# The running sum of the value rows in PSUM in the second pass, with 58 rows of the first kind ahead

## What is computed

```python
def peer(h, w_pq, sub_keys, u_tab, v_tab):
    ...
        expert = i0 * PEER_NKEYS + i1
        g = jax.nn.softmax(c_top, axis=-1)
        u = u_tab[expert]
        a = jax.nn.gelu(jnp.einsum('bthkd,btd->bthk', u, hb, preferred_element_type=jnp.float32),
                        approximate=False)
        return jnp.einsum('bthk,bthkd->btd', (g * a).astype(v_tab.dtype), v_tab[expert])
```

## Time and profile before

| | |
|---|---|
| median of 3 runs | 1715.59 us (1715.45 to 1722.47) |
| the profiled execution | 1718.16 us, its span from first to last instruction 1716.3 us |
| PE / DVE / POOL / ACT busy over the span | 88% / 68% / 41% / 28% |
| TensorE clock granted, mean | 0.966 |
| first pass | about 503 to 999 us |
| second pass | about 999 us to the end; gathered units from 1018 us |
| HBM read | 628.91 MB over the span |

### The profile page before, as it was taken

The page is one execution under the profiler, slowest core; times in us unless marked ns, Lnnn a source line. Parts: engine busy times, 40 slices in busy tenths (PEclk is TensorE's granted clock), DMA queues, the critical chain, the costliest instruction groups (busy, mean ns, idle before and its releaser), DMA issues.

```text
span 1716.3 us, 28250 instructions
## 1 busy us (share of the span) xinstructions
PE 1513.2 (88%) x11065; PEld 1412.6 (82%) x11065; DVE 1159.2 (68%) x1798; ACT 486.8 (28%) x1402; POOL 698.2 (41%) x420
## 2 busy tenths in 40 slices
PE   9999999999999999999999998777777776766766
PEld 7768888889999999999999998766777766766766
DVE  5335695767789999148676737666666666676766
ACT  6557567656540000034445481000000000000000
POOL 2020000000013222111001018888888888888885
PEclk9999999999999999999999999999888989999998
DMA  9664446476669999989999989998999999997887
GB/s 347 229 137 144 136 136 198 138 240 198 241 203 422 421 421 422 418 340 402 384 352 385 339 282 338 360 341 306 340 346 326 332 339 331 324 326 255 287 302 264
DMA packets 115092, 517.21 MB, mean 301 GB/s; under 512 B 25937, under 2 KB 28113, under 8 KB 62625
## 3 DMA queue, kind: packets, MB, share of 16 engines
q0 software_dynamic: 57488, 293.87, 47.0%
q1 hardware_dynamic: 48176, 156.19, 26.2%
q10 hardware_dynamic: 9360, 66.35, 9.7%
HBM read 628.91 MB, written 3.41 MB: 368 GB/s over the span
## 4 chain that ended last, share of the span: by engine, by line
PE 51%; POOL 17%; DMA 16%; issue 10%; DVE 4%; ACT 1%; POOLq 0%; DVEq 0%; SPq 0%; ACTq 0%
PE ps L1551 19%; DMA late<-in_u_tab 5%; PE ps L1335 5%; PE ps L1340 5%; PE ps L1337 5%; POOL late L498 5%; PE ps L1606 4%; POOL raw L516 3%; DMA late<-in_v_tab,acts 3%; POOL late L516 3%; POOL late L496 3%; DMA raw<-in_u_tab 3%; PE ps L1357 2%; POOL acts L498 2%; PE ps L1499 2%
## 5 line engine op out<-in xcount | busy, mean ns | idle before, releaser
L1606 PE MATMUL ps<-acts,raw 128*128 (+1 forms) x2048 | 266.7, 295 | 89.8 <-DMA raw<-in_v_tab,acts 89.5
L1606 PE MATMUL ps<-acts,late 128*128 (+1 forms) x2048 | 262.8, 291 | 90.4 <-DMA late<-in_v_tab,acts 90.4
L1606 PEld LDWEIGHTS ps<-acts,raw 128*128 128x128 f32 x2048 | 257.9, 209 | 98.1 <-issue 94.0
L1606 PEld LDWEIGHTS ps<-acts,late 128*128 128x128 f32 x2048 | 253.4, 205 | 98.4 <-issue 97.0
L846 DVE TENSOR_TENSOR w_lo<-raw,w_hi 128x512 fp32r<-128x512 f32 (+1 forms) x288 | 188.8, 682 | 131.3 <-ACT w_hi L540 129.7
L1161 DVE SCALAR_TENSOR_TENSOR late<-late,acts 128x2048 f32<-128x2048 f32 x85 | 194.2, 2293 | 96.6 <-DMA late<-in_u_rows,sel 95.8
L1165 DVE SCALAR_TENSOR_TENSOR acts<-late,sel,acts 128x2048 f32<-128x2048 f32 x85 | 200.2, 2355 | 65.4 <-DMA late<-in_v_tab,acts 61.8
L1551 PE MATMUL ps<-acts,late 128*128 128x128 f32 x2048 | 239.1, 276 | 5.6 <-DMA late<-in_u_tab 5.5
L1551 PEld LDWEIGHTS ps<-acts,late 128*128 128x128 f32 x2048 | 233.0, 192 | 8.4 <-DMA late<-in_u_tab 5.2
L1551 PE MATMUL ps<-acts,raw 128*128 128x128 f32 x1984 | 231.2, 276 | 3.1 <-DMA raw<-in_u_tab 2.8
L1551 PEld LDWEIGHTS ps<-acts,raw 128*128 128x128 f32 x1984 | 225.6, 192 | 5.8 <-DMA raw<-in_u_tab 4.7
(11 more groups left out here) (218 smaller groups left out, 1825.5 us busy)
## 6 DMA issues: line engine op xcount, KB each, us to landing
raw<-in_w_in SPq DMA_DIRECT2D x72, 512.0 KB, 3.7
late<-in_u_tab SPq DMA_DIRECT2D x33, 1024.0 KB, 10.8
raw<-in_u_tab SPq DMA_DIRECT2D x32, 1024.0 KB, 10.7
late<-in_u_tab ACTq DMA_DIRECT2D x31, 1024.0 KB, 10.8
raw<-in_u_tab ACTq DMA_DIRECT2D x30, 1024.0 KB, 10.5
raw<-in_w_o SPq DMA_DIRECT2D x32, 512.0 KB, 4.2
raw<-in_w_pq SPq DMA_DIRECT2D x32, 512.0 KB, 3.5
raw<-in_w_in SPq DMA_DIRECT2D x8, 400.0 KB, 3.4
```

Of the source, the lines that this page charges most:

```text
L1606: ins = mm(ps[:, pair_bank(k // 2), at:at + N_DN], ring[q][:, k * P:k * P + P], acts[:, ds(i * (4 * N_DN) + q * N_DN, N_DN)], start=first ...
```

## The change

The running sum moves from `acc` in SBUF to `held`, banks 0 to 3 of PSUM (2048 float32 per partition). The first value row reads `acc` and writes `held`; the last reads `held` and writes `acc`; the 126 between read and write `held`. The products of the rows of the first kind are written to SBUF as before. `U_FIRST` is 58 for 48, so that all rows ahead of the second pass are of the first kind; then 70 and 70 alternate, and 58 value rows stand at the end. PE's results of the second pass lie in banks 4 to 7 alone, 512 columns in each (`out_bank`), so that the first unit no longer waits in its middle; the copies, transposes and last sums go by banks, 4 for 8.

```diff
-        U_FIRST = 48
+        U_FIRST = 58
         ROWS = [("u", n) for n in range(U_FIRST)]
         for n in range(U_FIRST, N_PICK):
             ROWS += [("u", n), ("v", n - U_FIRST)]
         ROWS += [("v", n) for n in range(N_PICK - U_FIRST, N_PICK)]
         U_LAST = [ROWS.index(("u", TOPK * h + TOPK - 1)) for h in range(NH)]
         ROWS_U = 58
+        V_ROW = [ROWS.index(("v", n)) for n in (0, N_PICK - 1)]
...
-        def pair_bank(p):
-            return (p + 4) % 8
+        def out_bank(b):
+            return ps[:, 4 + b, :]
+
+        held = ps[:, 0:4, :].rearrange("p b n -> p (b n)")
...
             for n in range(4):
-                sp.wait_ge(out_ready, 2 * n + 2)
+                sp.wait_ge(out_ready, n + 1)
...
-            for p in range(KD // 2):
-                act.wait_ge(pair_mm, p + 1)
-                nc.scalar.activation(outT[:, 2 * p:2 * p + 2, :], ps[:, pair_bank(p), 0:2 * N_DN].rearrange("p (k t) -> p k t", k=2),
-                                     ACT.Copy).then_inc(outT_done, 1)
+            for b in range(KD // 4):
+                act.wait_ge(bank_mm, b + 1)
+                nc.scalar.activation(outT[:, 4 * b:4 * b + 4, :], out_bank(b).rearrange("p (k t) -> p k t", k=4), ACT.Copy).then_inc(outT_done, 1)
...
                         dve.wait_ge(row_used, r)
-                        V.scalar_tensor_tensor(acc, row[r % NROW], w_sp[:, n:n + 1], acc, ALU.mult, ALU.add).then_inc(row_used, 1)
+                        V.scalar_tensor_tensor(acc if r == V_ROW[1] else held, row[r % NROW], w_sp[:, n:n + 1], acc if r == V_ROW[0] else held, ALU.mult, ALU.add).then_inc(row_used, 1)
...
             apply(NKEY - 1)
 
+            dve.wait_ge(gelu_done, NKEY)
             next_row(3)
...
-            for p in range(KD // 2):
-                dve.wait_ge(outT_mm, p + 1)
-                cols = slice(256 * p, 256 * p + 256)
-                V.tensor_tensor(o_rest[:, cols], ps[:, pair_bank(p), 0:256], x_rest[:, cols], ALU.add).then_inc(out_ready, 1)
+            for b in range(KD // 4):
+                dve.wait_ge(outT_mm, b + 1)
+                cols = slice(512 * b, 512 * b + 512)
+                V.tensor_tensor(o_rest[:, cols], out_bank(b), x_rest[:, cols], ALU.add).then_inc(out_ready, 1)
...
                 for k in range(KD):
-                    if first and k == 8:
-                        pe.wait_ge(gelu_done, NKEY)
-                    at = N_DN * (k % 2)
-                    ins = mm(ps[:, pair_bank(k // 2), at:at + N_DN], ring[q][:, k * P:k * P + P], acts[:, ds(i * (4 * N_DN) + q * N_DN, N_DN)],
-                             start=first and k % 2 == 0, stop=last and k % 2 == 1)
+                    at = N_DN * (k % 4)
+                    ins = mm(out_bank(k // 4)[:, at:at + N_DN], ring[q][:, k * P:k * P + P], acts[:, ds(i * (4 * N_DN) + q * N_DN, N_DN)],
+                             start=first and k % 4 == 0, stop=last and k % 4 == 3)
```

More of the change, by code:

```diff
@@ L252, in build_block @@
         expert_in, used_done, unit_ready = sem("expert_in"), sem("used_done"), sem("unit_ready")
-        pair_mm, outT_done, outT_mm = sem("pair_mm"), sem("outT_done"), sem("outT_mm")
+        bank_mm, outT_done, outT_mm = sem("bank_mm"), sem("outT_done"), sem("outT_mm")
         out_ready, out_sent = sem("out_ready"), sem("out_sent")
@@ L1588, in _, with out_transposes @@
             pe.wait_ge(gated, N_GRP)
[L1589 to L1593, removed]
+            def out_transposes(b):
+                pe.wait_ge(outT_done, b + 1)
+                for k in range(4):
+                    ins = nc.tensor.transpose(out_bank(b)[:, P * k:P * k + P], outT[:, 4 * b + k, :], ident[:, :])
                 ins.then_inc(outT_mm, 1)
@@ L1602, in v_chunk @@
                 for k in range(KD):
-                    if first and k == 8:
-                        pe.wait_ge(gelu_done, NKEY)
-                    at = N_DN * (k % 2)
-                    ins = mm(ps[:, pair_bank(k // 2), at:at + N_DN], ring[q][:, k * P:k * P + P], acts[:, ds(i * (4 * N_DN) + q * N_DN, N_DN)],
-                             start=first and k % 2 == 0, stop=last and k % 2 == 1)
-                    if last and k % 2:
-                        ins.then_inc(pair_mm, 1)
-                        if k >= 5:
-                            out_transposes(k // 2 - 2)
+                    at = N_DN * (k % 4)
+                    ins = mm(out_bank(k // 4)[:, at:at + N_DN], ring[q][:, k * P:k * P + P], acts[:, ds(i * (4 * N_DN) + q * N_DN, N_DN)],
+                             start=first and k % 4 == 0, stop=last and k % 4 == 3)
+                    if last and k % 4 == 3:
+                        ins.then_inc(bank_mm, 1)
+                    if last and k in (9, 13):
+                        out_transposes(k // 4 - 2)
                 if not last:
@@ L1626, in _ @@
                 v_chunk(NKEY // 4 - 1, q, last=q == 3)
-            for p in range(KD // 2 - 2, KD // 2):
-                out_transposes(p)
+            for b in range(KD // 4 - 2, KD // 4):
+                out_transposes(b)
     return nc
```

## The result

The changed kernel takes 1592.5 us in the median (1588.1 to 1594.0), the kernel before beside it 1719.0. The ratio is 0.926, 95% interval 0.922 to 0.929: **7.4% faster**. Forecast were 1626 us and a range of 1590 to 1690, so the time lies in it, 2.5 us above its lower edge; the gain is 127 us where 93 were forecast.

What follows compares the result with a forecast made beforehand. POOL's issue rate was taken to bound the second pass; freed, DMA's 388 and DVE's 142 us make 530, with 12% loss 594. 1018 + 594 + 15 = 1627, forecast as a 1626 us median, range 1590 to 1690.

Steps and rivals of the forecast that it cites:

- The bound of before: Second pass, from 1018 us: POOL's issue rate bounds it, 320 instructions at one per 2.15 us.
- What holds POOL: Gathers issued inside DVE row instructions: a second SBUF input holds them; the changed sum has none, freeing 168 us of POOL.
- 1.40 us a row instruction: Second pass: each DVE product or sum with two SBUF inputs costs POOL 1.40 us over undisturbed gathers.
- The sum in PSUM for nothing: Value rows' sums on DVE: PSUM in place costs nothing, 2.44 us each; bounds 2.44 and 4.5 us.
- The rival with half of the rate: Sums in place in PSUM run at half rate, 4.5 us each, making DVE the bound: 1777 us, chance 0.06.
- The 65 ns more: Skill's higher fixed cost for PSUM on DVE: 65 ns x 128 = 8 us, doubted from the trace's 687 against 686 ns.
- What is late next: Second pass with POOL freed: DMA bounds the alternating part, 388 us, DVE the end, 142; 530 us together.
- the 12% for four servers that stall one another: Second pass: loss added to 530 us because POOL, DMA, DVE and PE stall each other, giving 594; bounds 5 to 20%.
- better than summed: Rival: losses under 5% and a full PE clock; at 4% 551 us for the second pass, 1583 in all; chance 0.06.
- The tail: End of the kernel, behind the second pass: 15 us, taken from 1701 to 1716 us of the kernel before.
- DMA early at 364 GB/s: Rival: DMA takes POOL's place in the second pass at a 364 GB/s ceiling, 1675 us, chance 0.16.
- Order, `gelu_done`, four banks: 58 rows ahead move nothing in the first pass; the gelu_done wait costs nothing; four output banks 0 to +1 us, taken as 0.

Runs made afterwards that it cites:

- pool_before2: Kernel before with a 256-column memset on POOL ahead of each of the 198 row gathers behind row 58; 1750.5 us, ratio 1.018.
- pool_after2: Changed kernel with a 256-column memset on POOL ahead of each of the 198 row gathers behind row 58; 1599.0 us, ratio 0.929.
- swap: Changed kernel with the running sum back in SBUF and the products' second operand hs read from PSUM from row 55 on; 1641.6 us, ratio 0.953.
- prod_out_psum: Changed kernel with the running sum in SBUF and products from row 55 on written to PSUM, both their inputs in SBUF; 1728.6 us, ratio 1.005.
- free_both_half: free_both with 4 KB gathered for each value row instead of 8; 1539.9 us, ratio 0.896.
- free_both: Changed kernel with products reading hs from PSUM, sums reading the same banks and writing acc, running sum left out; 1587.5 us, ratio 0.923.
- order58: Kernel before with only U_FIRST 58 for 48, the sum staying in SBUF; 1720.2 us, ratio 1.000.
- sum_sbuf: Changed kernel with the running sum back in SBUF for all 128 value rows; 1722.3 us, ratio 0.998.

## Why the prediction was right

- **The bound of before.** POOL's issue rate: right. Loading POOL by 42 us cost the kernel before 28 (22 to 40) and the changed one 6.5 (`pool_before2`, `pool_after2`).
- **What holds POOL.** From two rows, L1236 and L1220, the text took that a second tensor in SBUF does it. That was thin evidence, two places in one trace, and it held: `swap` shows it with the operands exchanged, `prod_out_psum` that the output has no part in it. The rule of the Trainium skill ("SBUF — State Buffer", section "Who interferes with whom") agrees with the traces of the two kernels, of `swap` and of `prod_out_psum`: a gather issued over 0.1 us into an instruction with two SBUF inputs takes 1.85 to 3.11 us before, and one issued inside an instruction with one such input at most 1.00 us in the others.
- **1.40 us a row instruction.** In the changed kernel 318 gathers cost POOL 11.25 + 304.87 + 99.19 = 415.3 us, so 415.3 - 318 x 0.98 = 103.7 over undisturbed ones, for 70 products: 1.48 each. 410 us were forecast.
- **The sum in PSUM for nothing.** 2355 ns in place, the lower bound of the two. The rival with half of the rate is out. The 65 ns more, the estimate from the Trainium skill's table of fixed costs ("VectorE: DVE Perf Modes", section on the TRN2 errata), did not appear.
- **What is late next.** DMA in the alternating part, 401 us (1018 to 1419) for the 388 of the sum; 402 GB/s for the 421 that were put in. DVE at the end: 150.5 us from 1419.2 to the last gather's end, for 142. Both servers were named rightly, and `free_both_half` shows both.
- **The term that was mis-sized is the 12% for four servers that stall one another.** Measured are (401 + 150.5) / 530 = 1.04. The text had 5% as the lower bound, for the first pass with the same buffers, and that was the better row, though still above what was measured. That six row buffers and four unit buffers are deep enough is how it looks; no run changed them. Two things go with it. PE, put in with 4.2 us a unit, came down: 310.07 / (2563 / 32) = 3.87, at a granted clock of 0.97 for 0.91, and it is busy 81% of the stretch for 74%. And a held POOL costs next to nothing while DMA is the bound (5 us, `free_both`). The loss of 22 us for 64 makes 42 us.
- **That the time lies in the range is in part luck.** A loss of 4% is outside the 5 to 20% that the range was made of; with it alone the prediction's own sum gives 1583 us, the number of its rival "better than summed", which had a chance of 0.06. What brought the time back to 1592.5 has nothing to do with the loss: 6 us more of tail, and a median 2 us above the span, where 1 below it had been put in. The mechanism, the bound of before and the two servers that came next were foreseen; how well the servers work side by side was not.
- **The tail** was set to 15 us and is 21: from the last gather's end at 1569.7 to 1590.5. Before, DVE waited for the data of the last gather; now it is still behind with an earlier sum when they land, as this timeline of DVE at the end shows (the last gather starts at 1568.70; compare):

```profile
1573.30 4.81 DVE L1167 SCALAR_TENSOR_TENSOR ps<-acts,sel,ps 128x2048 f32<-128x2048 f32 x2
1578.21 2.35 DVE L1167 SCALAR_TENSOR_TENSOR ps<-late,sel,ps 128x2048 f32<-128x2048 f32 x1
1580.67 2.35 DVE L1167 SCALAR_TENSOR_TENSOR acts<-late,sel,ps 128x2048 f32<-128x2048 f32 x1
1582.94 2.48 DVE L1309 TENSOR_TENSOR acts<-ps,acts 128x512 f32<-128x512 f32 x4
```

  Four sums stand without a gap. By the semaphore records of the trace the last row has landed at 1578.6, 8.9 us behind the end of its issue (before 1706.5, 5.3 us behind), and its sum starts 2.1 us later. Before, it started at once. Together, 3.6 and 2.0 us, these are the 6 us. 1018 + 551.5 + 21 = 1590.5 is the span, against 1018 + 594 + 15 = 1627: -42 for the loss, +6 for the tail.
- **DMA early at 364 GB/s**: out. Its share of 0.92 left more room than 8%: the rate rose by 20% (335 to 402) while the share rose by 9%. The trace has the other side of it: a packet of 8 KB took 354 ns in the mean from 1035 to 1533 us before and 321 from 1035 to 1419 now. Why it took longer at the lower rate was not tested. The 358 GB/s from HBM in the Trainium skill's table ("SBUF — State Buffer", section on the bandwidth-pool intuition) were passed for 384 us on end.
- **Order, `gelu_done`, four banks**: nothing, as summed (`order58`, `sum_sbuf`).

## What to carry to other kernels

Where GpSimd issues gathers beside VectorE, look at the minimum and the median of a gather's issue time. Here a median of twice the minimum was the sign that VectorE holds it, and the timeline says which instruction does. Moving one of that instruction's two tensor inputs to PSUM (here the second) freed the gathers and cost VectorE nothing, 2355 ns a sum in both places; the output can stay where it is. Before summing the gain, sum all the servers behind the freed one, in each part of the work: here POOL was freed of 172 us (698.2 - 526.3), and the kernel gained 127, because DMA's bytes and, at the end, DVE's sums came next.

## What was not expected of the hardware

- A short instruction on GpSimd between two gathers was free here: 0.12 us of memset lie within the 0.30 us that pass between two gathers anyway, and 198 of them changed neither kernel.
- DMA's busy share was no measure of what is left. At 0.92 it moved 335 GB/s, at 1.00 402.
- A gather that is issued in the first 0.09 us of a DVE instruction with two SBUF inputs mostly isn't held (19 of 21 in the kernel before); all that were issued later were held to its end, up to 3.11 us.
- A product that is written to PSUM (with its column sum to SBUF) needs 140 ns to read the sum out, for 82 ns when it is written to SBUF.
